# Weight sums of a fused LayerNorm with the weights stationary and four columns moving, and four waits in other places

## What is computed

```
h = x * (1 + scale) + shift
x = layernorm(ALPHA * x + w * gate * f(h)) * g + b
```

## Time and profile before

| | us |
|---|---|
| median of 3 runs | 954.46 (954.41 to 955.03) |
| the profiled execution | 954.59 |
| its span, first to last instruction | 952.8 |
| TensorE busy in it | 938.2 (98%) |
| VectorE, ScalarE, GpSimd busy | 506.4, 374.1, 267.6 |
| mean granted TensorE clock | 0.999 |

### The profile page before, as it was taken

The page is one execution under the profiler, slowest core; times in us unless marked ns, Lnnn a source line. Parts: engine busy times, 40 slices in busy tenths (PEclk is TensorE's granted clock), DMA queues, the critical chain, the costliest instruction groups (busy, mean ns, idle before and its releaser), DMA issues.

```text
span 952.8 us, 10887 instructions
## 1 busy us (share of the span) xinstructions
PE 938.2 (98%) x4233; PEld 757.7 (80%) x4233; DVE 506.4 (53%) x713; ACT 374.1 (39%) x567; POOL 267.6 (28%) x222
## 2 busy tenths in 40 slices
PE   8999999999999999999999999999999999999997
PEld 5788888888888888788767687888888888888886
DVE  6956767455464855777666488632232322233334
ACT  6752232232322313664586456532322323221224
POOL 0021111111105412337844575611111111125125
PEclk9999999999999999999999999999999999999999
DMA  9836565656644663122411121333223232213302
GB/s 359 364 131 201 185 209 181 200 175 211 198 152 143 224 226 113 70 89 89 133 66 45 45 69 66 111 111 108 91 93 107 89 98 95 83 64 120 119 20 88
DMA packets 38563, 127.21 MB, mean 134 GB/s; under 512 B 4080, under 2 KB 6256, under 8 KB 38512
## 3 DMA queue, kind: packets, MB, share of 16 engines
q1 hardware_dynamic: 38512, 126.52, 39.6%
HBM read 123.36 MB, written 2.10 MB: 132 GB/s over the span
## 4 chain that ended last, share of the span: by engine, by line
PE 92%; DVE 3%; POOL 1%; ACT 1%; DMA 1%; issue 1%; SPq 1%; POOLq 0%; DVEq 0%; ACTq 0%
PE bank L601 28%; PE bank L603 28%; PE bank L602 28%; PE bank L957 1%; PE bank L981 1%; DMA ada_first<-ada_w 1%; PE bank L968 1%; PE bank L686 1%; PE bank L687 1%; PE bank L680 1%; POOL cq L2015 0%; DVE w_lo L1081 0%; SPq L509 0%; DVE lat L1535 0%; PE bank L727 0%
## 5 line engine op out<-in xcount | busy, mean ns | idle before, releaser
L1081 DVE TENSOR_TENSOR w_lo<-raw,w_hi 128x1024 fp32r<-128x1024 f32 x153 | 206.2, 1355 | 278.4 <-ACT w_hi L1053 278.0
L601 PE MATMUL bank<-h_hi,w_hi 128*128 128x512 f32 x727 | 284.5, 391 | 0.0
L603 PE MATMUL bank<-h_hi,w_lo 128*128 128x512 f32 x727 | 283.0, 389 | 0.0
L602 PE MATMUL bank<-h_lo,w_hi 128*128 128x512 f32 x727 | 282.9, 389 | 0.0
L1053 ACT ACTIVATE w_hi<-raw 128x1024 fp32r<-128x1024 f32 x153 | 155.8, 1031 | 189.7 <-PE bank L603 188.2
L1917 POOL TENSOR_TENSOR a_lo<-act_t,a_hi 128x512 fp32r<-128x512 f32 x44 | 59.0, 1340 | 420.1 <-ACT a_hi L1175 420.1
L603 PEld LDWEIGHTS bank<-h_hi,w_lo 128*128 128x128 f32 x727 | 136.5, 188 | 28.6
L601 PEld LDWEIGHTS bank<-h_hi,w_hi 128*128 128x128 f32 x727 | 136.5, 188 | 28.4 <-issue 0.5
L602 PEld LDWEIGHTS bank<-h_lo,w_hi 128*128 128x128 f32 x727 | 136.6, 188 | 27.9
L601 PE MATMUL bank<-a_hi,w_hi 128*128 128x512 f32 (+1 forms) x374 | 141.2, 377 | 0.0
L602 PE MATMUL bank<-a_lo,w_hi 128*128 128x512 f32 (+1 forms) x374 | 140.8, 377 | 0.0
(11 more groups left out here) (304 smaller groups left out, 1044.6 us busy)
## 6 DMA issues: line engine op xcount, KB each, us to landing
raw<-wunits SPq DMA_DIRECT2D x145, 512.0 KB, 3.2
ada_ring<-ada_w SPq DMA_DIRECT2D x56, 512.0 KB, 4.3
ada_first<-ada_w SPq DMA_DIRECT2D x16, 512.0 KB, 11.0
raw<-wunits SPq DMA_DIRECT2D x16, 384.0 KB, 2.9
x<-xT SPq DMA_DIRECT2D x8, 256.0 KB, 5.1
outT<-x SPq DMA_DIRECT2D x8, 256.0 KB, 2.6
K<-k_rope SPq DMA_DIRECT2D x2, 512.0 KB, 8.1
c_act<-c_rows SPq DMA_DIRECT2D x1, 512.0 KB, 6.4
```

Source lines behind the costliest of these rows:

```text
L601: mm(out, lh, rh, start=first, stop=False)
L602: mm(out, lh, rl, start=False, stop=False)
L603: return mm(out, ll, rh, start=False, stop=last)
L1081: nc.vector.tensor_tensor(lo, raw[:, slot, 0:width], hi.bitcast(F32), SUB).then_inc(s_lo, 1)
```

## The change

The weight sums take the weights as stationary operand and the four columns of `gb` as the moving one; the results are columns at once, high and low parts apart, and VectorE adds and negates them. TensorE's three products, ScalarE's copy and the constant `sel` go; ScalarE's wait for the sums stays. Beside it, four steps move: one of GpSimd's shifts from step 30 to step 31, TensorE's wait for the last bank from ahead of the attention loop to step 3, VectorE's last split of the mixer behind the low parts of the sums, and the order of the last two stores is exchanged.

```
-SHIFTED_AFTER = {18: 0, 19: 1, 22: 4, 23: 5, 24: 6, 25: 7, 28: 2, 30: 3}
+SHIFTED_AFTER = {18: 0, 19: 1, 22: 4, 23: 5, 24: 6, 25: 7, 28: 2, 31: 3}
...
-        sel = sb("sel", [P, 2])
+        wfour = sb("wfour", [P, OPEN, 4])
...
             store(G_PE[1], 1, (s_hh[3], 5))
+            store(G_DVE, 1, (s_nx[3], 8))
             store(G_POOL, 1, (s_pf, 10))
-            store(G_DVE, 1, (s_nx[3], 8))
...
                     elif j == 1 and t == 2:
-                        pe.wait_ge(s_wc, 2)
+                        pe.wait_ge(s_wc, 6)
...
                 pe.wait_ge(s_lo, base + OPEN)
                 pe.wait_ge(s_gb, p)
-                out = bank[SUM_BANK[p]][0:4, 0:OPEN * P].rearrange("p (a b) -> p a b", b=P)
-                slots = slice(w_slot(base), w_slot(base) + OPEN)
-                for i, part in enumerate((w_hi, w_lo)):
+                for i in range(OPEN):
                     for k in range(KD):
-                        last = mm(out, gb[:, p - 1, k, :], part[:, slots, k * P:(k + 1) * P],
-                                  start=i == 0 and k == 0, stop=i == 1 and k == KD - 1)
+                        hi, lo = w(base + i, k * P)
+                        out = bank[SUM_BANK[p]][:, 4 * i:4 * i + 4]
+                        mm(out, hi, gb[:, p - 1, k, :], start=k == 0, stop=False)
+                        last = mm(out, lo, gb[:, p - 1, k, :], start=False, stop=k == KD - 1)
                 last.then_inc(s_r, 1)
-
-            def weight_columns(p):
-
-                pe.wait_ge(s_rc, p)
-                for i in range(OPEN):
-                    last = mm(bank[SUM_BANK[p]][:, 2 * i:2 * i + 2], s_sum[0:4, i * P:(i + 1) * P], sel[0:4, :],
-                              start=True, stop=True)
-                last.then_inc(s_sel, 1)
...
                     last.then_inc(s_used, 1)
-                    if j == 1:
-                        weight_columns(p)
...
                 if t == 5:
-                    pe.wait_ge(s_wc, 1)
+                    pe.wait_ge(s_wc, 3)
...
             emptied(pe, T_END - 2)
-            emptied(pe, T_END - 1)
...
+                if step == 3:
+                    emptied(pe, T_END - 1)
...
                         act.wait_ge(s_r, p)
-                        fn(s_sum[0:4, 0:OPEN * P], bank[SUM_BANK[p]][0:4, 0:OPEN * P], ACT.Copy).then_inc(s_rc, 1)
...
-                dve.wait_ge(s_sel, p)
-                cp(wcol[:, 0:2 * OPEN], bank[SUM_BANK[p]][:, 0:2 * OPEN]).then_inc(s_wc, 1)
-                dve.wait_ge(s_wc, p)
+                dve.wait_ge(s_r, p)
+                parts4 = bank[SUM_BANK[p]][:, 0:4 * OPEN].rearrange("p (n c) -> p n c", c=4)
+                pairs = wcol[:, 0:2 * OPEN].rearrange("p (n c) -> p n c", c=2)
+                cp(wfour[:], parts4).then_inc(s_wc, 1)
+                dve.wait_ge(s_wc, 3 * p - 2)
+                tt(pairs, wfour[:, :, 0:2], wfour[:, :, 2:4], ADD).then_inc(s_wc, 1)
+                dve.wait_ge(s_wc, 3 * p - 1)
+                ts(pairs[:, :, 0:1], pairs[:, :, 0:1], -1.0, None, MUL).then_inc(s_wc, 1)
+                dve.wait_ge(s_wc, 3 * p)
...
-            col(tt(sel[0:4, :], cols[0:4, C_ID:C_ID + 2], cols[0:4, C_ID + 2:C_ID + 4], ADD))
-            col(ts(sel[0:4, 0:1], sel[0:4, 0:1], -1.0, None, MUL))
...
                 mixer_residual(m)
-                lo_after(S_OUT + m - SPLIT_TILES)
+                if m < KD - 1:
+                    lo_after(S_OUT + m - SPLIT_TILES)
                 if m > SPLIT_TILES:
                     plain_low(2, m - 1)
             plain_low(2, KD - 1)
             sums_low(2)
+            lo_after(S_OUT + KD - 1 - SPLIT_TILES)
```

More of the change, by code:

```diff
@@ L251, in build @@
         gb = sb("gb", [P, 2, KD, 4], F32R)
-        sel = sb("sel", [P, 2])
-        margin2 = sb("margin2", [P, 142])
+        wfour = sb("wfour", [P, OPEN, 4])
+        margin2 = sb("margin2", [P, 132])
         ident = cols[:, C_ID:C_ID + P]
@@ L402, in build @@
         s_un = [None] + [sem(f"opening_normalised{p}") for p in range(1, 3)]
-        s_gb, s_r, s_rc = sem("gb_ready"), sem("weight_sums"), sem("weight_sums_copied")
-        s_sel, s_wc, s_evu = sem("weight_columns"), sem("weight_columns_copied"), sem("opening_scaled")
+        s_gb, s_r = sem("gb_ready"), sem("weight_sums")
+        s_wc, s_evu = sem("weight_columns"), sem("opening_scaled")
         s_silu = [sem(f"silu_done{f}") for f in range(2)]
```

## The result

The changed kernel takes 963.10 us (median of 6 runs, 959.88 to 963.57) against 954.43 us before on the same terms: ratio 1.0082, 95% interval 1.0073 to 1.0092. It is 8.7 us slower, where 0.8 us was forecast, and outside the range, which ended at 958.3.

A forecast was written before the change was run, and what follows sets the result against it. The prediction took TensorE, busy 98% of the span, as the bound. Terms +2.78 - 0.885 - 0.245 - 0.83 - 0.05 = +0.77 us gave 955.36, or 955.2 us as median; the 8-in-10 range was 953.8 to 958.3.

The forecast's parts named there:

- The whole sum: All terms for the whole kernel added, with TensorE's clock at 1.00: +0.77 us on the profiled execution's 954.59 us.
- Steps 1 to 3: Both openings: old weight sums and fp32 products removed (7.84 us), new narrow matmuls added (10.62 us), net +2.78 us.
- Step 3: New weight sums: 48 narrow matmuls per opening at 0.111 us each, 5.31 us per opening, 10.62 us for both.
- (b): In the new weight sums, each load-and-multiply pair costs more than its load, 0.13 to 0.19 us: 957.0 to 962.8; chance 10%.
- (c): In the new weight sums, loads take half the time, pace 0.055 us, giving 949.8 us; chance 3%.
- Steps 4, 6 and 7: Savings: VectorE's last split in opening 2, 0.885 us; GpSimd's last shift, 0.83; wait for the second Q head, 0.05.
- Rival (d): Other waits replace those removed at the split, the fifth unit and GpSimd's shift, so nothing is won: 957.2 us; chance 8%.
- step 7: Before the first attention scores: wait for the second Q head moved; of 0.34 us idle only about 0.05 saved.
- Step 5: Fifth unit of FFN 2: TensorE's wait for VectorE's split goes, saving 0.245 us.
- Step 8: Two tiny VectorE operations at 53 us and the exchange of the last two stores: no effect, 0.
- rival (a): TensorE's clock falls in the narrow stretch, 2.1 us lost per opening: 957.3 us for one, 959.4 for both; chance 12%.

## Why the prediction was wrong

The forecast was a sum with TensorE's clock at 1.00. Its terms held:

- *The whole sum.* With 128 columns moving, where the pace is the same and the clock stays up, the changed kernel stands at +0.56 us (-0.3 to +1.4) against +0.77 forecast.
- *Steps 1 to 3*, the net of the weight sums: not timed alone at full clock, but the kernel with 128 columns (955.18) less the one with the moves alone (952.63) is 2.55 us, where 2.78 - 0.245 = 2.54 was forecast.
- *Step 3*, the pace of a narrow pair: 0.111 us forecast, 0.11 us between the starts in the changed kernel for as long as the clock was up, 0.117 in the spread form. Rivals (b), dearer pairs, and (c), fast loads, are both out. The Trainium skill ("TensorE: Matmul & The Clock Gate", "Weight-path perf modes") has fast loads for 128 weights whose type is not FP32, and no gain for fp32. These fp32r weights are not loaded fast: loads of 128 columns keep 0.11 us from start to start.
- *Steps 4, 6 and 7*: 1.77 us forecast for the moves, 2.0 measured, with each of the two large ones shown alone. Rival (d) is out. Of step 7 the waits bear out the reading: the 0.3 us for which TensorE stood ahead of the first scores are gone, but its waits for ScalarE's `cq` went from 0.5 to 0.8 us.
- *Step 5*, the wait at the fifth unit: it is gone in the changed kernel, behind an opening in which TensorE was slowed by several microseconds, and just as much in the kernels with 128 columns, with spread matmuls and with groups of 16, whose clock stayed at 1.00. With the moves alone it is still there (0.4 us of idle loads above), as was expected of that run.
- *Step 8*, the stores and the two operations at 53 us: nothing of them shows; they were not tried alone.

**The step that failed is rival (a), TensorE's clock, which the sum put at nothing: its chance, 12%, and its price, 2.1 us for an opening.** It happened in both openings and cost about 4.9 and 3.3 us in the profiled execution. The chance rested on two arguments. One was that "TensorE's loads run without a gap in that stretch". The windows of the changed kernel have the loads busy for 5.00 of 5.00 us in the very stretch in which the clock falls, so loads are not what holds it. The other was that the clock held "through every stretch of transposes". That was no evidence: the transposes have 128 moving columns each (L968 in the earlier trace rows), and with 128 columns the clock held here too, while with 4, 32 and 64 it fell. The prediction had put the number that mattered, "4 columns in each 0.111 us, close to nothing", into the text and then weighed the wrong one. The Trainium skill, "TensorE: Matmul & The Clock Gate", Part 1, says that the gate follows how busy the engine has been. These runs add that the profile's busy share does not tell it: PE is listed as busy 5.00 of 5.00 us in every window above, in those with a clock of 1.00 and in those with 0.50.

The price failed because it took the 4.2 us of the kernel's first matmuls for the length of the low stretch. It lasted 10.3 us in opening 1 and 6.8 us in opening 2. In opening 1 the clock fell 2.4 us into the narrow matmuls; the 26 still to come then took 5.5 us instead of 2.9, and the clock came back only 4.7 us after the wide matmuls had begun again. So a fall that comes early also stretches the narrow matmuls still to come, which the price left out. The range, finally, reached only to a fall in one opening, though one cause acts on both.

What stays open is what sets the moment of the fall. In the changed kernel it came 2.4 us after the start of the narrow matmuls in opening 1 and 4.6 us in opening 2; in the kernel with the new sums alone, whose stretches start within 0.15 us of these, 4.6 and 3.3 us; and once, with groups of 24, 1 us after their end. So the place in the program does not decide it. That the moment moves from run to run would also account for the changed kernel's scatter over 3.7 us and that of the groups of 24 over 5.8, but only one execution of each kernel has a trace.

## What to carry to other kernels

Turning a product round so that a wide operand becomes stationary and four columns move saves no load time: each load of 128 columns takes 0.11 us, and four columns do not hide it. In an unbroken stretch it can also cost TensorE half its clock for several microseconds of dense work behind it: here in groups of 48, in some executions in groups of 24 (2.7 us), in none of ten in groups of 16 (1.8 us). If narrow matmuls can't be avoided, put them singly or in short groups between wide ones: here the kernels with the same 96 matmuls lie 1.1 us above the one before when these are spread and 8.7 when they are together. And when a change mixes parts, time them apart: the four moved steps were worth 2 us, and the change that carried them hid it.

## What was not expected of the hardware

A busy TensorE lost its clock. The profile showed 5.00 of 5.00 us busy for both matmuls and loads in the window in which the clock fell (0.73 on average), and 5.00 and 4.61 in the next, all of it at 0.50. Back-to-back loads of 128 columns with 4, 32 or 64 columns moving let it fall, with 128 moving it held, and so it did in 5.5 us of matmuls with four stationary and 384 moving columns. The fall can come after the cause is over (1 us after the last narrow matmul, in wide matmuls), so the row that is slow need not be the row that is to blame.
